# Mixture-of-experts layer: experts ranked by token count on the chip and run in 13 units instead of 16 fixed pairs

## The chip, the cores and the metric

The kernel runs on one core of a Trainium2 chip. The metric is the device time of one execution in microseconds (us); of a set of runs the median counts. The core has TensorE (matrix products; PE in the rows, with PEld for its weight loads), VectorE (DVE), ScalarE (ACT), GpSimd (POOL) and SyncE (SP, which here issues the large loads), and 16 DMA engines that carry all transfers.

## What is computed

One inference step of a two-layer network (`DEPTH = 2`) on 128 context tokens and 128 latent tokens. Each layer has a block of three token mixers, and then a mixture of 32 experts in which each of the 256 tokens goes to its 4 best experts. Only the second part is touched. All values are float32.

```python
D_MODEL, N_EXPERTS, TOP_K, D_EXPERT = 1024, 32, 4, 512

def _moe(h, p):
    t = h.reshape(b * n, d)
    logits = t @ p['router_w'] + p['router_b']
    top_v, top_i = lax.top_k(logits, TOP_K)
    w_top = jax.nn.softmax(top_v, axis=-1)
    combine = einsum('tk,tke->te', w_top, one_hot(top_i, N_EXPERTS))
    def expert(acc, e):
        w1, b1, w2, b2, ce = e
        gu = t @ w1 + b1                       # (1024 x 1024)
        gate = minimum(gu[:, :D_EXPERT], 7.0)
        up = clip(gu[:, D_EXPERT:], -7.0, 7.0)
        act = (up + 1.0) * (gate * sigmoid(1.702 * gate))
        return acc + ce[:, None] * (act @ w2 + b2), None   # w2: 512 x 1024
```

An expert's weights are 4 MB of w1 and 2 MB of w2. Every expert gets tokens, so all 32 are loaded in each layer.

## The kernel before

After the mixers, TensorE computes the router's logits; VectorE takes each token's four best experts, and from running counts the position of each token within each expert. Experts are worked through in **pairs**. A pair has 128 slots, 64 for each expert: a 0/1 matrix `S_s` (tokens by slots, made by `tokens_onehot`) gathers the tokens of both by matrix products (`gather`), and `SC_s` (from `combine_onehot`) scatters the weighted results back onto all tokens.

On TensorE one pair is, in `pair(q)`: products with the first half of w1 (L811, `part` 0, which counts up `g1_mm[0]`), with the second half (`part` 1, `g1_mm[1]`), the gather of the next pair (L770), four transposes of the activations (L819), the products with w2 (L837, `g2_mm`), the scatter (L845) and the next pair's biases (L778). The two experts of a pair lie in two column halves of the array: a weight tile is 128 rows by 64 slots, the expert's weights stream past it 512 columns at a time, and the halves of the two experts work at the same time.

An expert with more than 64 tokens gets further slots in an **extra** pair. VectorE finds these during pair 0 (L1542 to L1588: tables of 16 extras by 32 experts, in rows of 512 elements), and raises `routed`. The extra pairs run after the first three pairs, and the 13 fixed ones follow; the number of pairs is thus 16 and the extra ones, and all engines but SP run them in one hardware loop from pair 1 (TensorE from pair 2).

Weights come in **parts** of 2 MB: two of w1 and one of w2 for each expert, each of them one DMA issued by SP in program order. The buffers are the six slots of `ring`, which the mixers' weights use too: slots 0 and 1 for the first half of w1, 2 and 3 for the second, 4 and 5 for w2. SP waits on `g1_mm[0]`, `g1_mm[1]` or `g2_mm` before it issues the load into a slot that TensorE has finished with (`load_part`, L405). Two further buffers, `more`, hold the first halves of w1 of pair 1 once per layer. Eight parts are so loaded before pair 0 starts. At the end of a layer SP loads the next layer's first weights into the six slots as they come free.

Of the kernel before, what the change touches and what calls it, by code (L numbers as in the profile page):

```python
# [27 lines left out]
G = 2  # L28
# [13 lines left out]
FIRST = 3  # L42
# [17 lines left out]
C_PIDX, C_KK, C_EIDX, C_EPS, C_FOLD = 704, 705, 721, 753, 754  # L60
NC = 786
# [23 lines left out]
def merge_slot(kind, b, ch):  # L85

    return {"gate": S_WM[b][ch // 4], "proj": S_WO[b], "out": S_OUT + ch // 4}[kind]

# [6 lines left out]
def build(nc, x_in, cond_in, consts, vecs, rows, ada_w, w_in, w_q_b, w_kv_b, lru_gate_w, w_o_mla, w_o_lru,  # L95
# [3 lines left out]
    with ctx:  # L99
# [41 lines left out]
        eidi = sb("eidi", [P, MAX_EXTRA], I32)  # L141
        ps = ctx.enter_context(nc.psum_tensor("ps", [P, 8, 512], F32))

        def at(off, *dims):
# [8 lines left out]
            if len(dims) == 4:  # L153
# [61 lines left out]
        xtra = at(T0 + 436, N_EXP)  # L215
        tend = at(T0 + 468, N_EXP)
        tbeg = at(T0 + 500, N_EXP)
        npf = at(T0 + 532, 2)
        cmp8 = at(T0 + 534, 8)
        psub = at(T0 + 542, MAX_EXTRA)  # L220
        NTAB = N_EXP + MAX_EXTRA + 2
        pmT = at(T0 + 558, G, NTAB)
        cwT = at(T0 + 658, G, NTAB)
        eidf = at(T0 + 758, NTAB)
        ctT = at(T0 + 808, NT)
        lpart = ctT
        K0 = T0 + 1064
        sel, tmpx, tmpy = (at(K0 + 512 * i, MAX_EXTRA, N_EXP) for i in range(3))
        assert K0 + 3 * 512 <= 19776

# [34 lines left out]
                             "ct_mm", "ct_evac", "routed"))  # L265
        disp, xt_a, xt_v = (sem(n) for n in ("disp_rdy", "xt_evac_a", "xt_evac_v"))
# [101 lines left out]
        with nc.Fori(0, L) as l:  # L368
            with nc.Block() as block:

                @block.sync
                def _(sp_):
# [35 lines left out]
                    def pair(experts, waits, order=range(RING)):  # L408

                        srcs = [expert_parts(e) for e in experts]  # L410
                        for j in order:
                            s, v = waits[j]
                            sp_.wait_ge(s, v)
                            load_part(j, srcs[j % 2][j // 2])

                    def freed(pairs_before):

                        return [(g1_mm[0], pairs_before)] * 2 + [(g1_mm[1], pairs_before)] * 2 + \
                            [(g2_mm, pairs_before * 2)] * 2
# [5 lines left out]
                    free = [consumed(pos) for pos in last_pos]  # L425
                    pair((0, 1), free, order[:3])
                    sp_.wait_ge(pv_mm, 12)
                    sp_.wait_ge(out_done, 16 * 5)
                    load_part(1, expert_parts(3)[0], more[1], more_arr[1])
                    pair((0, 1), free, order[3:])  # L430
                    sp_.wait_ge(f_mm, len(MERGE))
                    sp_.wait_ge(f_dv, 32)
                    load_part(0, expert_parts(2)[0], more[0], more_arr[0])
# [4 lines left out]
                    sp_.wait_ge(routed, 1)  # L438
                    n_extra = sp_.value_load(meta[0:1, 0:1], min_val=0, max_val=MAX_EXTRA // 2)
                    with sp_.If(n_extra > 0):  # L440
                        with sp_.Fori(0, n_extra) as q:
                            e = [sp_.value_load(eidi[0:1, bass.ds(q * 2 + i, 1)], min_val=0, max_val=N_EXP - 1)
                                 for i in range(2)]
                            two = sp_.value_load(both[0:1, bass.ds(q, 1)], min_val=0, max_val=1)
                            with sp_.If(two > 0):
                                pair(e, freed(q + FIRST))
                            with sp_.Else():

                                srcs = expert_parts(e[0])
                                for j, (s, v) in enumerate(freed(q + FIRST)):  # L450
                                    sp_.wait_ge(s, v)
                                    if j % 2 == 0:
                                        load_part(j, srcs[j // 2])
                                    else:
                                        sp_.sem_inc(arr[j], 16)
# [1254 lines left out]
```

## Time and profile before

| | us |
|---|---|
| median of 3 runs | 1813.56 (1812.35 to 1814.66) |
| the profiled execution, own time | 1813.54 |
| its span in the trace | 1811.9 |
| TensorE busy | 1737.7 (96% of the span) |
| VectorE busy, ScalarE busy | 606.1, 275.9 |
| experts of layer 0, first product to last bias | 386.85 to 912.86 |
| experts of layer 1 | 1280.81 to 1804.98 |

The profile is of one execution. Times in the rows count from the span's start; the own time is 1.6 us longer than the span. Matrix products on TensorE are pipelined, so a row of the timeline that holds many of them is read by its start and by the start of the next row. In a row of products `128*64` is the weight tile, `128x512` the output. A product in float32 appears as two instructions.

### The profile page before, as it was taken

To read this page: it belongs to the slowest core of one execution; us is meant where nothing else is said; L and a number is where in the kernel's file an instruction comes from. 1 tells how busy PE (TensorE), PEld (TensorE's weight loads), DVE (VectorE), ACT (ScalarE), POOL (GpSimd) and SP (SyncE) were. 2 spreads that over 40 slices of the span, in tenths; PEclk is the share of its full clock that TensorE was granted. 3 is DMA by queue.
4 is the path that set the end of the run, shared out by engine and by line. 5 is a ranking of instruction groups with operands and counts; after the bars stand their busy time and mean duration, and the time that the engine had idled before them with its cause. 6 is when DMAs were issued, how large, how long until landed. Compare 5 with 4: busy or idle time off the path is not lost. (4 is left out here: it accounts for less than half of the span.)

```text
span 1811.9 us, 22234 instructions
## 1 busy us (share of the span) xinstructions
PE 1737.7 (96%) x8560; PEld 1002.6 (55%) x8560; DVE 606.1 (33%) x1733; ACT 275.9 (15%) x611; POOL 3.8 (0%) x6
## 2 busy tenths in 40 slices
PE   3999999989999999999979999999899999999998
PEld 1756787844444444444438468877544444444444
DVE  1368235261222222121233863443512121212122
ACT  2133222020000000000030422212100000000001
POOL 0000000000000000000000000000000000000000
PEclk9999999989999999999989999999999999999999
DMA  9754633956699999999976455368566999999994
GB/s 324 276 182 151 239 141 108 362 206 255 243 421 412 417 414 416 417 413 418 405 261 225 145 179 202 140 211 352 201 269 272 417 414 419 411 420 408 421 411 175
DMA packets 100557, 551.52 MB, mean 304 GB/s; under 512 B 12753, under 2 KB 15569, under 8 KB 75025
## 3 DMA queue, kind: packets, MB, share of 16 engines
q1 hardware_dynamic: 91376, 546.20, 75.8%
q10 hardware_dynamic: 9120, 4.53, 1.0%
q8 instruction: 36, 0.59, 0.1%
q14 instruction: 25, 0.20, 0.0%
HBM read 548.31 MB, written 2.40 MB: 304 GB/s over the span
## 5 line engine op out<-in xcount | busy, mean ns | idle before, releaser
L811 PE MATMUL ps<-ring,arena 128*64 128x512 f32 x2112 | 460.6, 594 | 0.0
L811 PEld LDWEIGHTS ps<-ring,arena 128*64 128x64 f32 x2112 | 148.7, 137 | 307.6 <-issue 306.1
L837 PE MATMUL ps<-ring,arena 128*64 128x512 f32 x1088 | 241.0, 595 | 0.0
L622 PE MATMUL ps<-hT,ring 128*128 128x256 f32 x768 | 171.4, 379 | 0.0
L770 PEld LDWEIGHTS ps<-arena 128*128 128x128 f32 x1152 | 139.1, 198 | 36.2 <-issue 26.0
L1518 DVE TENSOR_SCALAR arena<-cst,arena 128x64 f32<-128x64 f32 x136 | 33.4, 310 | 373.0 <-PE ps L811 372.9
L770 PE MATMUL ps<-arena 128*128 128x128 f32 x1152 | 148.5, 284 | 8.2 <-DVE arena L1508 8.2
L622 PEld LDWEIGHTS ps<-hT,ring 128*128 128x128 f32 x768 | 144.1, 190 | 19.4 <-issue 1.0
L837 PEld LDWEIGHTS ps<-ring,arena 128*64 128x64 f32 x1088 | 75.0, 137 | 141.7 <-issue 141.7
L622 PE MATMUL ps<-arena,ring 128*128 128x256 f32 x640 | 144.6, 380 | 2.9 <-ACT arena L1020 1.6
L1082 ACT ACTIVATE arena<-arena 128x512 f32<-128x512 f32 x34 | 21.4, 630 | 753.4 <-DVE arena L1596 753.4
L622 PEld LDWEIGHTS ps<-arena,ring 128*128 128x128 f32 x640 | 118.8, 190 | 19.0 <-issue 2.7
L845 PE MATMUL ps<-arena 128*128 128x256 f32 x544 | 126.5, 386 | 0.0
L583 PE MATMUL ps<-ring,hT 128*128 128x512 f32 (+1 forms) x320 | 121.4, 540 | 1.9 <-DVE hT L1182 1.9
L845 PEld LDWEIGHTS ps<-arena 128*128 128x128 f32 x544 | 100.5, 190 | 39.9 <-issue 27.6
L1608 DVE COPY arena<-ps 128x512 f32<-128x512 f32 x34 | 23.5, 692 | 222.8 <-PE ps L837 222.8
L583 PEld LDWEIGHTS ps<-ring,hT 128*128 128x128 f32 x320 | 58.0, 192 | 63.8 <-issue 62.5
L1596 DVE TENSOR_SCALAR arena<-ps 128x512 f32<-128x512 f32 x34 | 23.5, 691 | 149.4 <-PE ps L811 149.4
L492 PE MATMUL ps<-arena,cst 128*128 128x256 f32 x64 | 20.2, 485 | 38.9 <-PEq L334 28.3
L589 PE MATMUL ps<-hT,ring 128*128 128x256 f32 x256 | 55.6, 379 | 0.0
L589 PEld LDWEIGHTS ps<-hT,ring 128*128 128x128 f32 x256 | 48.5, 190 | 6.5
L999 ACT ACTIVATE arena<-ps,bmh 128x256 f32<-128x256 f32 x48 | 22.8, 475 | 142.4 <-PE ps L622 137.2
(266 smaller groups left out, 1317.3 us busy)
## 6 DMA issues: line engine op xcount, KB each, us to landing
ring<-exp_w_dram SPq DMA_DIRECT2D x194, 2048.0 KB, 10.9
ring<-ada_w_dram SPq DMA_DIRECT2D x24, 2048.0 KB, 8.6
ring<-w_in_dram SPq DMA_DIRECT2D x12, 2048.0 KB, 10.1
ring<-w_merge_dram SPq DMA_DIRECT2D x12, 2048.0 KB, 9.0
ring<-w_out_dram SPq DMA_DIRECT2D x4, 2048.0 KB, 10.9
arena<-exp_w_dram SPq DMA_DIRECT2D x4, 2048.0 KB, 20.0
ring<-w_o_lru_dram SPq DMA_DIRECT2D x2, 2048.0 KB, 7.7
ring<-w_o_mla_dram SPq DMA_DIRECT2D x2, 2048.0 KB, 19.3
```

The source lines that it names most:

```text
L583: last = mm(ps[:, bank, 0:w], hT[:, k, half * P:(half + 1) * P], slot[:, k, :], start=k == 0, stop=k == KC - 1)
L589: last = mm(ps[:, bank, c * NT:(c + 1) * NT], slot[:, k, ch * P:(ch + 1) * P], hT[:, k, :], start=k == 0, stop=k == KC - 1)
L622: last = mm(out, slot[:, k, cols], src[:, k, :], start=k == 0, stop=k == nk - 1)
L770: last = mm(ps[:, 2 + k // 4, (k % 4) * P:(k % 4 + 1) * P], X2[:, g, k * P:(k + 1) * P], S_s[:, g, :], start=g == 0, stop=g == 1)
L811: last = mm(ps[c, h, :], xTg[:, 4 * part + k, c], w[i][:, k, h * 512:(h + 1) * 512], start=False, stop=True, skip_group_check=True)
L837: last = mm(ps[c, 2 + h, :], actT[:, f, c], w[i][:, f, h * 512:(h + 1) * 512], start=f == 0, stop=f == 3)
L845: last = mm(ps[:, 4 + k // 2, (k % 2) * NT:(k % 2 + 1) * NT], O_s[:, k * P:(k + 1) * P], SCT[:, :], start=first and k % 2 == 0, stop=True, ...
L999: A(tg[:, ch, :], merge_ps(f), ACT.Tanh, bias=bmh[:, 8 * b + ch:8 * b + ch + 1], scale=0.5).then_inc(f_ac, 1)
L1082: A(sig_s, gate_s, ACT.Sigmoid, scale=ALPHA).then_inc(sig_a, 1)
L1518: V.tensor_scalar(SC_s[:, g, SLOTS * i:SLOTS * (i + 1)], cst[:, C_IOTA:C_IOTA + SLOTS], pmT[:, g, bass.ds(t + i, 1)], cwT[:, g, bass.ds(t ...
L1596: V.tensor_scalar(gate_s, ps[:, 0, :], LIMIT, None, ALU.min).then_inc(gate_v, 1)
L1608: V.tensor_copy(O_s[:, 512:1024], ps[:, 3, :]).then_inc(o_v, 1)
```

## The change

- The experts are taken by rank. Experts 0 to 3 keep fixed places, so that work can start before the ranks are known; the other 28 are ordered by token count, the fullest first (`ranks`, on VectorE, with `cnt` scaled and the expert's number as tie-breaker).
- `UNITS` lists 13 units: nine pairs of 64 slots each, one unit of 96 and 32 slots (the fullest ranked expert and the last one), and three units of four experts with 32 slots each. A unit still has 128 slots. Units 0 to 11 are written out one after another on every engine; unit 12 and the extras run in the hardware loop. Extras come last, after unit 12.
- In units with 32 or 96 slots the array is split into four column groups of 32 (`tiles`); the group of an expert streams that expert's weights. With 96 slots three groups stream the same weights.
- The ring has eight buffers (six slots and `more`); part n goes into buffer n mod 8, and SP waits for the use of part n - 8. From unit 2 on SP reads the expert's number from `eidi` into a register before the unit's loads, after `routed`. In unit 12 and the extras the parts use slots 2 and 3, 4 and 5, 0 and 1.
- The tables of positions and weights by rank are no longer built on VectorE in 512-element rows but by small matrix products with a selection matrix `selT`: `table_parts` stands between the two halves of w1 of unit 0, `tables` behind the second. The transposition of the combine weights (L786 before) is in `table_parts`, so the biases of unit 0 follow the gather directly. TensorE waits for `routed` before the scatter of unit 0.
- `tokens_onehot` and `combine_onehot` take one operation each for all equal-sized experts of a unit; `combine_onehot` multiplies `S_s` by the weights.

```diff
+UNITS = (pair_at(0), pair_at(2), ((4, 96), (31, 32)), pair_at(5), pair_at(7), quad_at(19), pair_at(9), pair_at(11),
+         quad_at(23), pair_at(13), pair_at(15), quad_at(27), pair_at(17))
+NU = len(UNITS)
+CAPACITY = [w for _, w in sorted(e for unit in UNITS for e in unit)]
+LOOPED = NU - 1
+PARTS = [(u, kind, i) for u, unit in enumerate(UNITS[:LOOPED]) for kind in range(3) for i in range(len(unit))]
+BUFS = RING + 2
+LOOP_SLOTS = ((2, 3), (4, 5), (0, 1))
...
+                    def part_freed(n):
+                        u, kind, _ = PARTS[n]
+                        sp_.wait_ge(*((g1_mm[0], u + 1), (g1_mm[1], u + 1), (g2_mm, 2 * u + 2))[kind])
+                    def load_static(n, e):
+                        b = n % BUFS
+                        if n >= BUFS:
+                            part_freed(n - BUFS)
+                        src = part_source(PARTS[n][1], e)
+                        if b < RING:
+                            load_part(b, src)
+                        else:
+                            load_part(b, src, more[b - RING], more_arr[b - RING])
...
-                    pair((4, 5), freed(1), (0, 1))
-                    pair((2, 3), freed(1), range(2, RING))
-                    pair((4, 5), freed(2), range(2, RING))
+                    sorted_from = part_number(2, 0, 0)
+                    for n in range(BUFS, sorted_from):
+                        load_static(n, fixed_expert(n))
                     sp_.wait_ge(routed, 1)
+                    for u in range(2, LOOPED):
+                        ids = [sp_.value_load(eidi[0:1, t:t + 1], min_val=0, max_val=N_EXP - 1) for t, _ in UNITS[u]]
+                        for kind in range(3):
+                            for i, e in enumerate(ids):
+                                load_static(part_number(u, kind, i), e)
...
+                    def tiles(u):
+                        widths = [w for _, w in UNITS[u]]
+                        if widths == [SLOTS, SLOTS]:
+                            return [(i, slice(SLOTS * i, SLOTS * (i + 1))) for i in range(2)]
+                        owner = [i for i, w in enumerate(widths) for _ in range(w // 32)]
+                        return [(i, slice(32 * n, 32 * n + 32)) for n, i in enumerate(owner)]
...
+                    for u in range(LOOPED):
+                        experts = tiles(u)
+                        w1_products(u, 0, experts, part_weights(u, 0))
+                        if u == 0:
+                            table_parts()
+                        w1_products(u, 1, experts, part_weights(u, 1))
+                        if u == 0:
+                            tables()
+                        pe.wait_ge(disp, u + 2)
+                        gather(range(6))
+                        act_transposes(u)
+                        w2_products(u, experts, part_weights(u, 2))
+                        if u == 0:
+                            pe.wait_ge(routed, 1)
+                        scatter(u, first=u == 0)
+                        biases()
```

The order of instructions shows three places. On TensorE, first the start of unit 0 in each layer. Before: the gather of pair 0, the transposition of the combine weights (L786), the biases, all 32 products with w1, the next gather.

```order
L770 MATMUL ps<-arena 128x128 x16
L786 MATMUL ps<-cst,arena 32x128 x2
L778 MATMUL ps<-arena 128x512 x2
L811 MATMUL ps<-ring,arena 64x512 x32
L770 MATMUL ps<-arena 128x128 x12
```

After, down to the gather of unit 1 (L827 is the gather, L835 the biases, L849 the products with w1, L917 to L926 `table_parts`, L934 to L941 `tables`):

```order
L835 MATMUL ps<-arena 128x512 x2
L849 MATMUL ps<-ring,arena 64x512 x16
L917 MATMUL ps<-cst,arena 32x128 x2
L919 MATMUL ps<-cst,arena 32x128 x2
L925 MATMUL ps<-arena,cst 32x1 x2
L926 MATMUL ps<-arena,cst 128x1
L849 MATMUL ps<-ring,arena 64x512 x16
L934 MATMUL ps<-arena 128x50
L936 MATMUL ps<-arena,cst 128x16
L934 MATMUL ps<-arena 128x50
L936 MATMUL ps<-arena,cst 128x16
L939 MATMUL ps<-arena 128x50 x2
```

Two products have left the place ahead of the biases, and fourteen small ones (with L941 behind the last row) stand within and behind the products with w1. Second, on TensorE, a whole pair before (pair 1), in the same names:

```order
L811 MATMUL ps<-arena 64x512 x16
L811 MATMUL ps<-ring,arena 64x512 x16
L770 MATMUL ps<-arena 128x128 x12
L819 MATMUL ps<-cst,arena 128x128 x4
L770 MATMUL ps<-arena 128x128 x4
L824 MATMUL ps<-cst,arena 128x128 x2
L837 MATMUL ps<-ring,arena 64x512 x16
L845 MATMUL ps<-arena 128x256 x8
L778 MATMUL ps<-arena 128x512 x2
```

After, unit 2, the first with column groups of 32:

```order
L849 MATMUL ps<-ring,arena 32x512 x32
L849 MATMUL ps<-arena 32x512 x32
L827 MATMUL ps<-arena 128x128 x12
L858 MATMUL ps<-cst,arena 128x128 x4
L827 MATMUL ps<-arena 128x128 x4
L863 MATMUL ps<-cst,arena 128x128 x2
L873 MATMUL ps<-ring,arena 32x512 x32
L885 MATMUL ps<-arena 128x256 x8
L835 MATMUL ps<-arena 128x512 x2
```

Only the counts of L849 and L873 double, with half the columns each; a unit of four experts has the same rows. Third, on SP, the loads around the wait for `routed`. Before, these are the last parts of pairs 1 and 2:

```order
L405 ISA [waits w1_mm1]
L405 DMA ring<-exp_w1_dram 128x4096
L405 ISA [waits w2_mm]
L405 DMA ring<-exp_w2_dram 128x4096
L405 ISA [waits w2_mm]
L405 DMA ring<-exp_w2_dram 128x4096
L439 TENSOR_LOAD meta [waits routed]
L439 ISA x2
```

After, the last part of unit 1 and the first three of unit 2:

```order
L432 ISA [waits w1_mm1]
L432 DMA ring<-exp_w2_dram 128x4096
L481 TENSOR_LOAD eidi [waits routed]
L481 ISA x2
L481 TENSOR_LOAD eidi
L481 ISA x2
L432 ISA [waits w2_mm]
L432 DMA ring<-exp_w1_dram 128x4096
L432 ISA [waits w2_mm]
L432 DMA ring<-exp_w1_dram 128x4096
L432 ISA [waits w1_mm0]
L432 DMA arena<-exp_w1_dram 128x4096
```

The wait for `routed` has moved ahead of the loads of unit 2, register loads stand ahead of each unit's parts, and a part waits for whichever stage used its buffer last (here w1 parts wait for `w2_mm`).

## Rows read from the trace of the kernel before

**Rows 1.** Page, part 1: span; part 5: one group that runs once a pair.

```profile
span 1811.9 us, 22234 instructions
...
L1608 DVE COPY arena<-ps 128x512 f32<-128x512 f32 x34 | 23.5, 692 | 222.8 <-PE ps L837 222.8
```

**Rows 2.** Timeline of TensorE, one pair (start, duration, line, shape, count).

```profile
579.33 13.95 PE L811 MATMUL ps<-ring,arena 128*64 128x512 f32 x64
593.21 2.94 PE L770 MATMUL ps<-arena 128*128 128x128 f32 x24
...
597.91 7.09 PE L837 MATMUL ps<-ring,arena 128*64 128x512 f32 x32
604.93 3.72 PE L845 MATMUL ps<-arena 128*128 128x256 f32 x16
...
609.64 13.96 PE L811 MATMUL ps<-ring,arena 128*64 128x512 f32 x64
```

**Rows 3.** Waits of SP's queue: total us, times, longest.

```profile
SPq L405 <- PE ps L811: 564.7, 62, 30.8
```

**Rows 4.** Loads at L405: issue times, and times from issue to landing.

```profile
L405 SPq DMA_DIRECT2D ring<-exp_w_dram x2: 333/333/333, 605.2 to 605.7; - x2
...
DMA to landing us min/median/max: 8.7/10.9/13.1
...
L405 SPq DMA_DIRECT2D ring<-exp_w_dram x2: 333/333/333, 617.0 to 617.6; - x2
...
DMA to landing us min/median/max: 7.6/9.8/11.9
```

**Rows 5.** Stretches: length, busy times, granted clock, DMA share, GB/s (last three columns).

```profile
823.10:853.40 30.30, 30.30 (x156) 14.35 (x154) 6.69 (x17) 2.21 (x4) 0.00 (x0) 1.00 1.00 415
...
505.00:520.00 15.00, 15.00 (x74) 7.58 (x75) 2.19 (x4) 0.98 (x2) 0.00 (x0) 1.00 1.01 434
0.00:20.00 20.00, 0.00 (x0) 0.00 (x0) 0.61 (x3) 3.30 (x3) 0.20 (x4) 1.00 0.94 328
```

**Rows 6.** Page, part 6: issues of expert weights, KB each, us to landing.

```profile
ring<-exp_w_dram SPq DMA_DIRECT2D x194, 2048.0 KB, 10.9
...
arena<-exp_w_dram SPq DMA_DIRECT2D x4, 2048.0 KB, 20.0
```

**Rows 7.** Timeline of TensorE: the modulation products of layer 1, in four column groups.

```profile
929.67 7.08 PE L501 MATMUL ps<-ring,cT 128*32 128x512 f32 x64
```

**Rows 8.** Timeline of TensorE, pair 0 and the start of pair 1, layer 0.

```profile
384.62 0.62 PE L786 MATMUL ps<-cst,arena 128*32 128x128 f32 x4
385.79 1.13 PE L778 MATMUL ps<-arena 32*128 32x512 f32 x4 [0.55 <-ACT arena L1071]
386.85 13.95 PE L811 MATMUL ps<-ring,arena 128*64 128x512 f32 x64
403.27 4.45 PE L770 MATMUL ps<-arena 128*128 128x128 f32 x24 [2.46 <-DVE arena L1508]
...
420.87 4.44 PE L858 MATMUL ps<-arena 32*128 32x256 f32 x16
425.23 9.60 PE L811 MATMUL ps<-arena 128*64 128x512 f32 x32
```

**Rows 9.** Stretches in pairs 0 and 1 of layer 0; columns as in rows 5.

```profile
400.00:405.00 5.00, 2.54 (x12) 1.74 (x9) 4.16 (x16) 0.63 (x1) 0.00 (x0) 0.80 1.00 429
...
425.00:430.00 5.00, 5.00 (x13) 1.48 (x14) 0.00 (x0) 0.00 (x0) 0.00 (x0) 0.50 0.64 272
```

**Rows 10.** Timeline of VectorE, first operation behind a register load.

```profile
400.77 0.18 DVE L1586 COPY arena<-cst 128x26 f32 x1 [1.07 <-issue]
```

**Rows 11.** Timeline of TensorE: last biases of layer 0, first and last rows of layer 1's experts.

```profile
911.73 1.13 PE L778 MATMUL ps<-arena 32*128 32x512 f32 x4
...
1280.81 13.95 PE L811 MATMUL ps<-ring,arena 128*64 128x512 f32 x64
...
1803.85 1.13 PE L778 MATMUL ps<-arena 32*128 32x512 f32 x4
```

More of the change, by code:

```diff
@@ L406, in load_part, with part_source @@
                             arr[slot] if signal is None else signal, 16)
[L408 to L419, printed above, removed]
+                    def part_source(kind, e):
+                        return expert_parts(e)[kind]
@@ new lines, in w1_products @@
+                    def w1_products(q, part, experts, weights):
+                        for k in range(4):
+                            for h in range(2):
+                                for i, c in experts:
+                                    last = mm(ps[c, h, :], xTg[:, 4 * part + k, c],
+                                              weights[i][:, k, h * 512:(h + 1) * 512], start=False,
+                                              stop=True, skip_group_check=True)
+                        last.then_inc(g1_mm[part], 1)
@@ L863, in _ @@
-                    with pe.Fori(2, pairs) as q:
-                        pair(q)
+                    for u in range(LOOPED):
[14 more added lines that the diff above has]
+                        biases()
+                        if u == 0:
+                            pe.wait_ge(ld_b2, 16)
+                            for k in range(KC):
+                                mm(ps[:, 4 + k // 2, (k % 2) * NT:(k % 2 + 1) * NT], b2[0:N_EXP, k * P:(k + 1) * P],
+                                   ctT[0:N_EXP, :], start=False, stop=True, skip_group_check=True)
@@ new lines, in _ @@
+                    with pe.Fori(LOOPED, pairs) as q:
+                        experts = tiles(LOOPED)
+                        w1_products(q, 0, experts, loop_weights(q, 0))
+                        w1_products(q, 1, experts, loop_weights(q, 1))
+                        pe.wait_ge(disp, q + 2)
+                        gather(range(6))
+                        act_transposes(q)
+                        w2_products(q, experts, loop_weights(q, 2))
+                        scatter(q)
+                        biases()
@@ L1087, in pair @@
                         A(O_s[:, 0:512], ps[:, 2, :], ACT.Copy).then_inc(o_a, 1)
[L1089 removed]
+                    for u in range(LOOPED):
+                        pair(u)
                     act.wait_ge(routed, 1)
[L1091 to L1092 removed]
+                    pairs = act.value_load(meta[0:1, 1:2], min_val=NU, max_val=NU + MAX_EXTRA // 2)
+                    with act.Fori(LOOPED, pairs) as q:
                         pair(q)
```

379 lines of the change are left out of this document (217 added, 162 removed).

## The prediction

> **What bounds the kernel now.** I read the page first, for how often the expert work runs: the copy at L1608 stands once in a pair, and it ran 34 times [rows 1], so each layer has 17 pairs, 16 fixed and one extra. Then the timeline of one pair [rows 2]: the rows on TensorE join without a gap, 13.95 us for w1, then 4.7 us to the start of w2 (w1 ends at 593.2, w2 starts at 597.9), 7.0 for w2, 4.7 for scatter and biases (604.9 to 609.6). From start to start it is 30.31 us. TensorE never waits there for a load; SP waits for TensorE, 564.7 us in all for w1 products [rows 3]. So TensorE sets the pace. The loads, though, are close behind. Each expert part of 2 MB is 2.097 million bytes; two parts issued at 605.2 and 605.7 landed 8.7 and 13.1 us later, at 613.9 and 618.8, and the next two, issued at 617.0 and 617.6, at 624.6 and 629.5 [rows 4]. With a queue, landings are 4.9 us apart (428 GB/s); the part issued at 617.0 found the queue nearly done and began 2.7 us after its issue (624.6 - 4.9 = 619.7), which leaves a hole of 0.9 us. Six parts thus take 29.4 us of a pair's 30.3. The whole pair shows 415 GB/s at a DMA share of 1.00 [rows 5], because TensorE asks for no more. Taking work off TensorE is worth little more than 3% of a pair before the loads take over; taking loads away is worth more.
>
> **What is loaded and run.** 194 + 4 parts were issued [rows 6]: 66 experts, 33 per layer, so each extra pair holds one expert. The router of the reference, worked out for the reference's own inputs, agrees: in layer 0 only expert 1 (76 tokens) exceeds 64, in layer 1 only expert 29 (80). By rank, expert 29 gets the unit with 96 slots and needs no extra. Expert 1 is one of the four with a fixed place, and keeps its extra. No expert in a 32-slot place has more than 27 tokens, none in a 64-slot place more than 60 apart from expert 1. So layer 0 goes from 17 units to 14, layer 1 from 17 to 13, and the loads from 66 experts to 65.
>
> **A unit of four experts on TensorE.** It has twice the weight tiles of a pair, with half the columns. The nearest row is the modulation, the same shape with four different weight streams: 64 products in 7.08 us [rows 7], 110 ns each, against 13.95/64 = 218 ns for two streams [rows 2]. So 128 products take 14.1 us as a pair's 64 take 13.95, and I give all units 30.31 us, 13 x 30.31 = 394 us for a layer. Their loads do not shrink: 12 parts x 4.9 = 58.8 us for four experts. **The bound changes from TensorE to the loads.** What the three large units save on TensorE becomes waiting there, and the pairs between let the loads run ahead by what eight buffers hold.
>
> **The head of unit 0.** L786 and its wait leave the place before the biases: these start when L786 did, 384.62 instead of 385.79 [rows 8], 1.2 us earlier in each layer. In pair 0 the gather waited 2.46 us for VectorE's tables and then took 4.45 us instead of 2.94 at a granted clock of 0.80 [rows 8, 9]; that goes. In its place stand 14 small products. L786's four instructions are two such, 0.62 us, so 14 x 0.31 = 4.3 us; the bounds are 0 (beside VectorE's activation chain) and 8.6 (the same at half clock). VectorE's rank chain, some 15 operations of about 0.2 us, lies under the first half of w1. The b2 products (4.4 us) and the slow 9.60 us behind them, at a clock of 0.50, remain [rows 8, 9]. The register loads on SP, about 1.07 us each [rows 10], lie in its waits; four before a large unit are 4.3 us while several parts are queued, so I charge nothing. If that cover is gone, they become the rival below. The one-hots fall from ten operations to three a unit on VectorE, which is off the path: no gain.
>
> **The sum for one layer.** I walk through the parts: a part begins when the one before it has landed, or 3.0 us after the use of its buffer ends (0.3 to the issue, 2.7 to the start), whichever is later. Eight parts lie ready. Counted from the first w1 product of unit 0:
> - Part 14 needs the buffer of part 6, which unit 1's first half of w1 uses: 30.3 (unit 0) + 4.3 (small products) + 4.4 (b2) + 2.6 (slow clock, 9.60 less 7.0) + 7.0 + 3.0 = 51.6. The parts 8 to 13 have landed before.
> - From there to part 89, the last of unit 11, are 76 parts x 4.9 = 372.4 us, with four holes of 0.9 while units 1 to 4 are still paced by TensorE as now: 427.6.
> - Then the tail: 0.1 to the wake-up, 7.0 for w2, 1.5 for the low clock after the wait (the 4.45 less 2.94 above), 4.7 for scatter and biases, and unit 12, whose parts have landed meanwhile, 30.3: **471.3 us**.
>
> Layer 0 adds its extra behind that, 30.3, loaded under unit 12: 501.6. Before, layer 0 took 386.85 to 911.73 + 1.13, which is 526.0; layer 1 1280.81 to 1803.85 + 1.13, 524.2 [rows 8, 11]. The gain is 24.4 + 52.9, and 2 x 1.2 at the heads: 79.7 us. What lies around (the update of x, the next layer's first loads) stays. The profiled execution's own time is 1813.54, 1.6 us over its span and equal to the median of 1813.56. **Forecast: 1734 us.**
>
> Ends of the terms: at 434 GB/s, as 15 us of rows 5 show, a part takes 4.83 us, -7 us in all after the longer holes; at the pair's 415 it takes 5.05, +16. I take 4.9, the spacing of landings itself. The small products move it by -9 to +9. Quad stages longer by a quarter, from starting after each wait at a low clock as in rows 9, cost +17. Together about 1718 to 1760.
>
> **A rule against this.** Expert loads moved at 434 GB/s for 15 us on end [rows 5]. The Trainium skill (DMA: Bandwidth & Descriptors, "Where 436 GB/s comes from") says that transfers from HBM to SBUF are bound at about 358 GB/s per core. By it, an estimate, a part takes 5.86 us, a layer some 74 us more, and the change ends near 1880, slower than before. The trace already runs above that figure, so the measurement decides; a rate that falls in longer stretches stays as a rival.
>
> **The rivals.**
> - *The large units take longer on TensorE.* If four column groups run only two abreast (218 ns as in rows 2), or every stage behind a wait stays at half clock, w1 and w2 take 21 us more in each of the four units with groups of 32. The same walk then gives 34 us more per layer: 1802. Against it speaks the 110 ns of rows 7; for it, that TensorE now waits some 20 us in a large unit. Half that effect gives 1769. The Trainium skill (TensorE: Matmul & The Clock Gate, "HAM oscillation — how this bites in real kernels") describes groups of products that each start cold after a wait for a DMA; rows 9 show one such case, and the sum has it once, at the end. 10%, most of it at the half effect.
> - *Not four groups side by side at all: slower.* Then a 32-column product costs 2 x 218 = 436 ns, and w1 and w2 of such a unit 63 us more. TensorE alone needs 13 x 30.31 + 4 x 63 + 11.3 = 657 us in a layer: 1734 + 2 x 186 = 2106. It turns slower once a unit takes 57 us, which is 248 ns a product. Rows 7 are against it. 1%.
> - *The loads do not hold 4.9 us without a pause: slower.* The opening 20 us moved only 328 GB/s at a share of 0.94 [rows 5], though in smaller pieces; that is 6.39 us a part. Per layer 76 x 1.49 - 3.6 + 8 (unit 12 waits too) = 118: 1969. The point is 5.47 us a part (383 GB/s), where 2 x (76 x 0.57 - 3.6) eats the 79.7. Expert parts stand at 415 to 434. 3% beyond the point, 2% between 5.1 and it (1755 to 1810).
> - *The ranking doesn't remove layer 1's extra*, by a wrong place or capacity: one unit of 30.3 us back, 1764. The counts say no. 4%.
> - *Register loads come into the open* on SP: 28 in a layer x 1.07 = 30 us, 1794 if nothing covers them. SP sits waiting most of a pair today. 2%.
>
> **How the numbers follow.** The forecast with its terms' bounds, 1718 to 1760, has 78%. The range needs 80% and takes in the half effect of the first rival and the extra: 1718 to 1769. A measurement of this kernel can tell 0.2% from no change, 3.6 us. All cases end faster but the two slower ones (4%); nearly none falls within 0.2% (1%). Faster 95%.
>
> **What would show it.** Right: 27 executions of the pair's copy instead of 34 (14 + 13) and 195 expert parts; four-group products at about 110 ns; from unit 5 on waits of TensorE for loads, some 20 us in a large unit and none in unit 12, and DMA at about 428 GB/s without a hole; layers of about 502 and 471 us. Wrong: a mean near 218 ns; TensorE without waits in the large units; holes between parts behind register loads; a rate under 400 GB/s while parts are queued.

## The result, and the profile after

The changed kernel takes 1729.94 us (median of four runs, 1728.60 to 1733.86) against 1813.01 for the kernel before in the same comparison: a ratio of 0.9544, with a 95% interval of 0.9527 to 0.9561. It is 83.1 us faster. The forecast was 1734.0, a gain of 79.7. The profiled execution took 1728.60 us, with a span of 1726.9.

The page of the changed kernel, parts 1, 2, 5 and 6, to be held against [rows 1, 6]:

```profile
span 1726.9 us, 20608 instructions
PE 1556.0 (90%) x8298; PEld 905.1 (52%) x8298; DVE 514.6 (30%) x1415; ACT 260.9 (15%) x585; POOL 3.8 (0%) x6
...
GB/s 336 294 159 144 295 69 130 355 187 321 419 419 412 428 426 428 427 427 427 317 261 313 150 152 269 70 156 324 218 298 412 420 412 427 428 427 428 428 427 200
...
L1763 DVE COPY arena<-ps 128x512 f32<-128x512 f32 x27 | 18.7, 692 | 228.2 <-PE ps L873 228.2
...
ring<-exp_w_dram SPq DMA_DIRECT2D x151, 2048.0 KB, 20.6
...
arena<-exp_w_dram SPq DMA_DIRECT2D x44, 2048.0 KB, 15.6
```

The copy at L1763 stands once in a unit and ran 27 times, 14 + 13, in place of 34 [rows 1]. 151 + 44 = 195 expert parts were issued in place of 198 [rows 6], and the usual time from issue to landing has grown from 10.9 to 20.6 us: a longer queue of loads now stands before the DMA engines. The GB/s row shows it: in each layer's expert work (slices 11 to 19 and 31 to 39) it climbs from 412–420 to 426–428 and stays there.

The waits, TensorE's and those of SP's queue (total us, times, longest), beside [rows 3]:

```profile
PE ps L849 <- DMA ring<-exp_w_dram: 66.2, 10, 11.3
PE ps L873 <- DMA ring<-exp_w_dram: 37.6, 6, 7.5
...
SPq L432 <- PE ps L849: 523.6, 50, 29.1
...
SPq L481 <- DVE eidi L1737: 4.4, 2, 2.2
```

Before, TensorE did not wait for an expert load at all. Now it waits 66.2 + 37.6 = 103.8 us for w1 parts (L849) and w2 parts (L873). SP's wait for the ranked ids (L481) comes once in a layer and is short.

The timeline of TensorE in layer 0 (start, duration, line, operation, shape, count, and in brackets the idle time before it and what ended it): unit 2, the first with four column groups, which finds its weights ready; unit 8, the second large unit behind the first pairs; the end of unit 11 and the start of unit 12:

```profile
450.10 7.07 PE L849 MATMUL ps<-ring,arena 128*32 128x512 f32 x64
456.99 7.05 PE L849 MATMUL ps<-arena 128*32 128x512 f32 x64
...
650.56 1.07 PE L849 MATMUL ps<-arena 128*32 128x512 f32 x2 [2.92 <-DMA ring<-exp_w_dram]
...
670.14 8.76 PE L849 MATMUL ps<-ring,arena 128*32 128x512 f32 x64 [9.57 <-DMA ring<-exp_w_dram]
...
689.94 1.06 PE L873 MATMUL ps<-arena 128*32 128x512 f32 x2 [6.32 <-DMA ring<-exp_w_dram]
...
703.67 13.95 PE L849 MATMUL ps<-ring,arena 128*64 128x512 f32 x64
...
808.94 1.07 PE L873 MATMUL ps<-arena 128*32 128x512 f32 x2 [6.08 <-DMA ring<-exp_w_dram]
...
818.20 3.72 PE L885 MATMUL ps<-arena 128*128 128x256 f32 x16
...
822.91 13.95 PE L849 MATMUL ps<-ring,arena 128*64 128x512 f32 x64
```

Unit 2: 128 instructions with 32 columns take 14.1 us, 110 ns each, just as a pair's 64 take 13.95. (The prediction counts instructions as products; a product in float32 is two of them.) Unit 2 holds two experts, of 96 and 32 slots, and so two weight streams. Four streams stand first in unit 5; its first half of w1, which finds its weights ready, in the line view (count, ns min/median/max, first and last start):

```profile
L849 PE MATMUL ps<-arena x32: 592/592/617, 541.0 to 547.5; 128*32 128x512 f32 x32
...
L849 PE MATMUL ps<-ring,arena x32: 592/592/617, 541.0 to 547.5; 128*32 128x512 f32 x32
```

These 64 instructions take 7.1 us, again 110 ns each. Unit 8 waits three times, 2.92 + 9.57 + 6.32 = 18.8 us; unit 11 waits 22.2 in the same way. The pair behind each runs without a wait, unit 12 too. That is the pattern of the forecast, but for unit 5, which waits only 10.1 us.

The loads, first as stretches (columns as in [rows 5]; the last three are granted clock, DMA share, GB/s), then as issues at L432 with their times to landing, which answer to [rows 4]:

```profile
590.00:700.00 110.00, 91.19 (x531) 40.50 (x528) 17.18 (x30) 6.63 (x12) 0.00 (x0) 0.89 1.01 427
700.00:800.00 100.00, 83.90 (x470) 37.84 (x469) 14.20 (x26) 5.04 (x9) 0.00 (x0) 0.93 1.01 428
```

```profile
L432 SPq DMA_DIRECT2D ring<-exp_w_dram x2: 332/332/333, 717.8 to 718.3; - x2
...
DMA to landing us min/median/max: 26.9/29.1/31.3
...
L432 SPq DMA_DIRECT2D arena<-exp_w_dram x2: 332/332/333, 729.5 to 730.1; - x2
...
DMA to landing us min/median/max: 24.9/27.1/29.3
```

These four parts land at 744.7, 749.6, 754.4 and 759.4: 4.9 us apart, without the hole of 0.9 that the prediction read from [rows 4]. TensorE is busy 91 of 110 us, the DMA engines all the time. The bound has passed from TensorE to the loads.

The ends of the layers on the same timeline, answering to [rows 8, 11]:

```profile
383.01 7.09 PE L849 MATMUL ps<-ring,arena 128*64 128x512 f32 x32
...
882.48 1.13 PE L835 MATMUL ps<-arena 32*128 32x512 f32 x4
...
1249.54 7.09 PE L849 MATMUL ps<-ring,arena 128*64 128x512 f32 x32
...
1718.80 1.13 PE L835 MATMUL ps<-arena 32*128 32x512 f32 x4
```

From the first w1 product to the end of the last bias, layer 0 takes 883.61 - 383.01 = 500.6 us and layer 1 takes 1719.93 - 1249.54 = 470.4. The forecasts were 501.6 and 471.3, the times before 526.0 and 524.2.

### The profile page after: what moved, and what is told of

It reads as the page before. It is cut to its first block and busy times, and to the rows that moved or that the text cites. A ratio compares the mean times of both kernels' runs of the same rounds, so it can differ in the third digit from the quotient of the medians.

```text
span 1726.9 us, 20608 instructions
## 1 busy us (share of the span) xinstructions
PE 1556.0 (90%) x8298; PEld 905.1 (52%) x8298; DVE 514.6 (30%) x1415; ACT 260.9 (15%) x585; POOL 3.8 (0%) x6
## 5 line engine op out<-in xcount | busy, mean ns | idle before, releaser
L849 PE MATMUL ps<-ring,arena 128*64 128x512 f32 (+1 forms) x1856 | 371.2, 632 | 50.4 <-DMA ring<-exp_w_dram 50.4
L849 PEld LDWEIGHTS ps<-ring,arena 128*64 128x64 f32 (+1 forms) x1856 | 111.9, 132 | 266.2 <-issue 266.2
L679 PE MATMUL ps<-hT,ring 128*128 128x256 f32 x768 | 171.4, 379 | 0.0
L873 PE MATMUL ps<-ring,arena 128*64 128x512 f32 (+1 forms) x736 | 161.9, 634 | 0.0
L679 PEld LDWEIGHTS ps<-hT,ring 128*128 128x128 f32 x768 | 144.1, 190 | 19.4 <-issue 1.0
L873 PE MATMUL ps<-arena 128*32 128x512 f32 (+1 forms) x384 | 98.2, 670 | 37.6 <-DMA ring<-exp_w_dram 37.6
L827 PEld LDWEIGHTS ps<-arena 128*128 128x128 f32 x928 | 111.5, 197 | 23.5 <-issue 20.5
L827 PE MATMUL ps<-arena 128*128 128x128 f32 x928 | 119.0, 283 | 2.6 <-DVE arena L1650 2.6
L1657 DVE TENSOR_TENSOR arena<-arena 128x256 f32<-128x256 f32 (+2 forms) x29 | 11.6, 407 | 318.1 <-PE ps L849 318.1
L885 PE MATMUL ps<-arena 128*128 128x256 f32 x432 | 100.5, 386 | 0.0
L885 PEld LDWEIGHTS ps<-arena 128*128 128x128 f32 x432 | 79.8, 190 | 31.9 <-issue 22.1
L849 PE MATMUL ps<-arena 128*32 128x512 f32 (+1 forms) x384 | 79.1, 642 | 15.8 <-DMA ring<-exp_w_dram 15.8
L1763 DVE COPY arena<-ps 128x512 f32<-128x512 f32 x27 | 18.7, 692 | 228.2 <-PE ps L873 228.2
L873 PEld LDWEIGHTS ps<-arena 128*32 128x32 f32 (+1 forms) x384 | 27.7, 135 | 99.0 <-issue 99.0
L873 PEld LDWEIGHTS ps<-ring,arena 128*64 128x64 f32 (+1 forms) x736 | 45.7, 131 | 62.5 <-issue 62.5
L849 PEld LDWEIGHTS ps<-arena 128*32 128x32 f32 (+1 forms) x384 | 21.5, 122 | 70.5 <-issue 70.5
## 6 DMA issues: line engine op xcount, KB each, us to landing
ring<-exp_w_dram SPq DMA_DIRECT2D x151, 2048.0 KB, 20.6
```

The source lines that it names most:

```text
L679: last = mm(out, slot[:, k, cols], src[:, k, :], start=k == 0, stop=k == nk - 1)
L827: last = mm(ps[:, 2 + k // 4, (k % 4) * P:(k % 4 + 1) * P], X2[:, g, k * P:(k + 1) * P], S_s[:, g, :], start=g == 0, stop=g == 1)
L849: last = mm(ps[c, h, :], xTg[:, 4 * part + k, c], weights[i][:, k, h * 512:(h + 1) * 512], start=False, stop=True, skip_group_check=True)
L873: last = mm(ps[c, 2 + h, :], actT[:, f, c], weights[i][:, f, h * 512:(h + 1) * 512], start=f == 0, stop=f == 3)
L885: last = mm(ps[:, 4 + k // 2, (k % 2) * NT:(k % 2 + 1) * NT], O_s[:, k * P:(k + 1) * P], SCT[:, :], start=first and k % 2 == 0, stop=True, ...
L1763: V.tensor_copy(O_s[:, 512:1024], ps[:, 3, :]).then_inc(o_v, 1)
```

## The experiments

The theory: from about unit 5 on the loads set the pace; a part costs 4.9 us; what the large units save on TensorE comes back as waits, as far as the ring's look-ahead doesn't carry the savings over to the next pairs. The rivals that the trace alone does not exclude: the ranking does all of it and the large units nothing; the gain hangs on something else, register loads or clock; the waits are a thing of the places that the large units stand in. All ratios are against the kernel before. Layer times are read as above, from each kernel's profiled execution; waits are TensorE's for expert loads, both layers together. x_halfw2 and x_noreg do not compute the reference's output.

| kernel | median us | ratio (95%) | layer 0 | layer 1 | waits |
|---|---|---|---|---|---|
| before | 1813.01 | 1 | 526.0 | 524.2 | none |
| after | 1729.94 | 0.9544 (0.9527–0.9561) | 500.6 | 470.4 | 103.8 |
| x_pairs | 1771.45 | 0.9770 (0.9754–0.9786) | 521.9 | 491.6 | none |
| x_six | 1797.23 | 0.9906 (0.9889–0.9923) | 533.8 | 504.1 | 167.8 |
| x_halfw2 | 1646.57 | 0.9083 (0.9057–0.9108) | 458.7 | 428.4 | 41.2 |
| x_noreg | 1729.39 | 0.9535 (0.9520–0.9551) | 500.6 | 470.9 | 106.1 |
| x_b2late | 1723.66 | 0.9498 (0.9485–0.9511) | 497.3 | 467.5 | 101.0 |
| x_order | 1723.09 | 0.9495 (0.9482–0.9508) | 501.2 | 467.4 | 100.5 |
| x_warm | 1727.52 | 0.9521 (0.9508–0.9534) | 498.9 | 469.4 | 93.8 |
| x_all | 1715.16 | 0.9447 (0.9434–0.9460) | 492.9 | 462.5 | 82.5 |
| a_again (after once more) | 1730.84 | 0.9542 (0.9529–0.9555) | 500.6 | 470.8 | 105.6 |
| b_again (before once more, one execution) | 1812.86 | – | 524.4 | 525.9 | none |

**Ranking without large units.** The table of units holds pairs only, 16 in a layer; slots, ranking and ring stay.

```diff
-UNITS = (pair_at(0), pair_at(2), ((4, 96), (31, 32)), pair_at(5), pair_at(7), quad_at(19), pair_at(9), pair_at(11),
-         quad_at(23), pair_at(13), pair_at(15), quad_at(27), pair_at(17))
+UNITS = (pair_at(0), pair_at(2), ((4, 96), (31, 32))) + tuple(pair_at(t) for t in range(5, 31, 2))
```

> The changed kernel with a different table of units: ranks, ring of eight and everything else kept, but 16 units (two fixed pairs, the one of 96 and 32 slots, thirteen pairs) and no unit of four experts. Theory of the prediction (units of four shift the bound from TensorE to the loads): TensorE sets the pace again at 30.31 us a unit, 17 units in layer 0 and 16 in layer 1, no waits for loads; about 24 us more per layer than the changed kernel, 1777 us. Rival (the gain came from the ranks' missing extra, the head of unit 0 and the larger ring, and the units of four only trade work for waits): within 8 us of the changed kernel, 1722 to 1738.

It took 1771.45, and both layers are 21 us longer than after, where 24 was expected. The GB/s row of this kernel's page:

```profile
GB/s 333 283 182 144 260 120 98 394 166 358 417 412 421 411 419 412 420 408 348 259 260 302 156 144 286 94 100 392 163 358 420 409 422 409 420 412 419 413 373 119
```

The rate in the expert work is that of a pair before [rows 5], 408 to 422 GB/s, and no wait for a load stands in the list of TensorE's waits: TensorE sets the pace again. Its layer 1 can be added up from pieces: 16 units of 30.31 [rows 2], 3.1 for the small products and 3.5 for b2 (both as measured after, see below) are 491.6, the time measured. So the change's 83 us are two halves: 41.6 us from ranking and what comes with it (32.6 us of that in layer 1, whose extra unit is gone; 4.1 in layer 0, where only pair 0's wait with its slow gather and the slow clock behind b2 could go; the rest lies ahead of the layers and between them), and 41.5 us from the large units. The eight buffers were not taken out of this kernel by themselves; but TensorE waited for no load with six before, so pairs alone leave them little to give. The rival that the ranking does it all falls.

**Six buffers in place of eight.** The ring keeps its six places; the two further buffers and the two parts loaded ahead into them go.

```diff
-BUFS = RING + 2
-LOOP_SLOTS = ((2, 3), (4, 5), (0, 1))
+BUFS = RING
+LOOP_SLOTS = ((0, 1), (2, 3), (4, 5))
...
-                    load_static(RING + 1, fixed_expert(RING + 1))
...
-                    load_static(RING, fixed_expert(RING))
```

> The changed kernel with the ring cut from eight buffers to the six slots (the two further buffers unused, eight parts ready at the start become six). Theory (loads bound the units of four, and the ring decides how far they run ahead): while four parts of a unit of four are in use only two buffers can fill, holes appear between the loads; the same walk through the parts gives 29 us more per layer, about 1788 us. Rival (the ring only matters for the start; six slots were enough before): about 10 us more per layer at most, 1730 to 1750.

It took 1797.23: both layers are 33 us longer than after, where 29 was expected. TensorE's waits, and one stretch in layer 0 (columns as above):

```profile
PE ps L847 <- DMA ring<-exp_w_dram: 113.9, 19, 13.8
PE ps L871 <- DMA ring<-exp_w_dram: 53.9, 6, 9.8
```

```profile
700.00:760.00 60.00, 49.88 (x298) 25.28 (x292) 10.47 (x17) 4.42 (x8) 0.00 (x0) 0.94 0.94 388
```

The waits grow by 64 us, and in the stretch the rate falls to 388 GB/s at a DMA share of 0.94: the loads pause. Work and units are the same, so 67 of the 83 us are lost without the longer look-ahead. Six buffers with large units are slower even than eight with pairs alone (1797 against 1771); six with pairs alone were not run. Why the loss was 33 and not 29 a layer wasn't followed further.

**Half of each w2 part not loaded.** In units 2 to 11 only the first half of the w2 matrix is loaded (the products run unchanged on what lies in the buffer), so the loads shrink and TensorE's work does not.

```diff
+                        if PARTS[n][1] == 2 and PARTS[n][0] >= 2:
+                            half = src.rearrange("o (p k) n -> p (o k) n", p=P)[:, 0:2, :]
+                            dst = ring[:, b, 0:2048] if b < RING else more[b - RING][:, 0:2048]
+                            sp_.dma_start(dst.rearrange("p (k n) -> p k n", k=2), half).then_inc(
+                                arr[b] if b < RING else more_arr[b - RING], 16)
+                            return
```

> The changed kernel with only the first half of each w2 part loaded in units 2 to 11 (the output is then not the reference's). Theory (loads are the bound from unit 5 on): waits of TensorE for loads nearly vanish, 43 us less per layer, about 1644 us; TensorE's own work, 13 x 30.3 us and the head of unit 0, is the floor near 1630. Rival (units of four are long on TensorE itself, or the clock after waits holds it back): within 10 us of the changed kernel.

It took 1646.57; the layers fall by 41.9 and 42.0 us, against an expected 43. TensorE's waits for loads, in this kernel:

```profile
PE ps L855 <- DMA ring<-exp_w_dram: 41.2, 11, 8.3
```

The waits fall from 103.8 to 41.2 and the time by 83.4 us with not one product less: the waits of TensorE are the loads', and bytes are what sets the end. The other 21 us is TensorE's busy time in the layers, which falls from 867.2 to 845.8 for the same instructions, because fewer stages run at the lower clock (mean granted clock 0.97 and 0.98 in place of 0.94). That the waits nearly vanish was a miss: 41.2 us are left.

**No register loads.** In units 2 to 11 the ids of the experts come from the table of places in place of a load from SBUF into SP's registers (so the routed units load experts by place and not by rank, as many bytes).

```diff
-                        ids = [sp_.value_load(eidi[0:1, t:t + 1], min_val=0, max_val=N_EXP - 1) for t, _ in UNITS[u]]
+                        ids = [t for t, _ in UNITS[u]]
```

> The changed kernel with the register loads of the experts' numbers in units 2 to 11 left out on SP: the loads take experts by their place in the table instead of by rank (the output is then not the reference's). Theory of the prediction (register loads lie in SP's waits and cost nothing): within 3 us of the changed kernel. Rival (they delay the issue of loads): 26 fewer per layer at about 1 us each, up to 50 us less, 1680 us.

It took 1729.39 against 1729.94, layers of 500.6 and 470.9. The register loads cost nothing that can be measured; SP has time for them behind the queued parts, as it sits 523.6 us in its waits for w1 products.

**The b2 products later.** The 16 small products that add b2 move from unit 0, where TensorE sets the pace, to unit 5.

```diff
-                        if u == 0:
+                        if u == 5:
```

> The changed kernel with the 16 products with b2 moved from behind unit 0 to behind unit 5, the first unit of four. Theory (units 0 to 4 are paced by TensorE and hold the buffers, from unit 5 on the loads set the pace, so TensorE's work costs its full time before unit 5 and nothing after): 3.5 us less per layer, about 7 us less in all, 1723 us. Rival (the loads set the pace from the start of the experts, or TensorE does throughout): no difference, within 2 us.

It took 1723.66, 3.3 and 2.9 us less per layer than after where 3.5 was expected. On the timeline of this kernel the products have their old length at the new place:

```profile
582.22 3.61 PE L965 MATMUL ps<-arena 32*128 32x256 f32 x16
```

There they don't make the layer longer: TensorE's waits are 2.8 us less and its busy time 3.4 us less, both layers together. In unit 0 they delayed the release of the buffers, and with it every part behind: part 14 lands 48.2 us after the first w1 product in layer 0, in place of 51.8 after.

**The large units earlier.** The units of four stand at places 2, 5 and 11 in place of 5, 8 and 11, so that the loads set the pace from the third unit on.

```diff
-UNITS = (pair_at(0), pair_at(2), ((4, 96), (31, 32)), pair_at(5), pair_at(7), quad_at(19), pair_at(9), pair_at(11),
-         quad_at(23), pair_at(13), pair_at(15), quad_at(27), pair_at(17))
+UNITS = (pair_at(0), pair_at(2), quad_at(19), ((4, 96), (31, 32)), pair_at(5), quad_at(23), pair_at(7), pair_at(9),
+         pair_at(11), pair_at(13), pair_at(15), quad_at(27), pair_at(17))
```

> The changed kernel with the units in another order: units of four experts at places 2, 5 and 11 instead of 5, 8 and 11. Theory (total loads decide, the order only sets how many holes the loads have while TensorE paces them): 2 to 3 us less per layer, about 1725 us. Rival (the spacing of units of four is what lets the loads run ahead; two of them close together wait in full): about 10 us more per layer, 1750 us.

It took 1723.09, where 1725 was expected. Fewer holes are in the loads: added up from the landings of parts 15 to 89, the pauses beyond 4.89 us a part are 3.8 and 4.3 us in the two layers, against 7.0 and 6.7 after. In the profiled execution, its slowest at 1727.13, layer 1 is 3.0 us shorter than after and layer 0 is 0.6 longer. The timeline and a stretch of layer 0 of this execution account for that:

```profile
417.00 4.95 PE L965 MATMUL ps<-arena 32*128 32x256 f32 x16
421.88 9.09 PE L849 MATMUL ps<-arena 128*64 128x512 f32 x32
```

```profile
420.00:425.00 5.00, 5.00 (x13) 1.99 (x13) 0.00 (x0) 0.00 (x0) 0.00 (x0) 0.50 0.87 374
```

The clock fell to half (0.50, the level of 1.2 GHz) during and behind the b2 products, which made these two rows 4.95 and 9.09 us long in place of 3.61 and 7.09: 3.3 us. That is the slow clock of [rows 8, 9], which the execution of after did not have; without it, an estimate, the layer would be 2.7 shorter than after.

**Work in the last wait.** Before the w2 products of unit 11, whose wait for loads is the last in the trace after, TensorE multiplies data that nobody reads.

```diff
+                        if u == LOOPED - 1:
+                            pe.wait_ge(sct_ev, u + 1)
+                            for _ in range(6):
+                                mm(ps[:, 1, :], ident, X2[:, 0, 0:512], start=True, stop=True, skip_group_check=True)
```

> The changed kernel with six products whose result nobody uses (128 columns of weights, 512 columns of data, 5 us in all) in front of the w2 products of unit 11, where TensorE waits some 6 us for a load. Theory (behind that wait w2 runs at the low clock and takes 9.2 us instead of 7.0, and this is the last wait, so it counts): w2 there 7.0 us, 2 us less per layer, 1726 us. Rival (the time is decided by the loads up to the end, so the clock costs nothing): no difference, within 1.5 us.

It took 1727.52. First the line view of the w2 products of unit 11 after (count, ns min/median/max, first and last start) and a stretch in it; then the same of this kernel, with the filling products above:

```profile
L873 PE MATMUL ps<-ring,arena x32: 592/592/1062, 809.0 to 817.7; 128*32 128x512 f32 x32
...
810.00:815.00 5.00, 5.00 (x35) 1.31 (x28) 0.00 (x0) 0.10 (x1) 0.00 (x0) 0.65 1.00 419
```

```profile
804.84 5.42 PE L960 MATMUL ps<-arena,cst 128*128 128x512 f32 x12 [0.47 <-ACT arena L1213]
...
L873 PE MATMUL ps<-ring,arena x32: 592/592/617, 810.2 to 816.7; 128*32 128x512 f32 x32
...
810.00:815.00 5.00, 5.00 (x49) 1.56 (x52) 0.00 (x0) 0.60 (x1) 0.00 (x0) 1.00 1.00 423
```

The stage takes 7.0 us in place of 9.3, and the granted clock in it is 1.00 in place of 0.65: an engine that has worked until the load lands starts at full clock. The stage's gain is plain, 2.3 us in layer 0 and 2.6 in layer 1. The layers, though, are only 1.7 and 1.0 us shorter than after. Part of the gain comes back in unit 12, which has a wait that after did not have:

```profile
829.62 7.09 PE L849 MATMUL ps<-ring,arena 128*64 128x512 f32 x32 [0.62 <-DMA ring<-exp_w_dram]
```

After, the second of the two parts that this half needs landed at 828.2 and TensorE came to it at 829.9, so there were 1.7 us to gain before the loads bind again. In the whole kernel the gain is at the edge of what can be told: 0.9521 (to 0.9534) against 0.9542 (from 0.9529) for after in its second comparison.

**All three edits** (b2 late, large units early, work in the last wait).

> The three edits before this one together: b2 behind unit 5, units of four at places 2, 5 and 11, six unused products before w2 of unit 11. If they add: 7 + 5 + 4 us less than the changed kernel, about 1714 us. Rival (the first two fill the same holes in the loads): about 1720 us.

It took 1715.16 us, a ratio of 0.9447 (0.9434 to 0.9460) against the kernel before and 0.9% under the changed kernel; layers of 492.9 and 462.5. The three gains, each against after in ratio times 1813 (8.0, 8.5 and 3.8 us), add up to 20; together they give 17. It is the fastest version of this study that loads every weight; the GB/s row of its page:

```profile
GB/s 334 302 151 154 261 67 171 305 241 311 418 428 428 428 428 427 427 427 427 333 261 314 159 154 245 67 186 287 259 295 408 427 427 428 428 427 428 427 427 219
```

The rate is at 427–428 from the twelfth slice on, two slices earlier than after.

**Both kernels once more.** In the first traces the router of layer 0 ended 3 us earlier after than before, ahead of anything that the change touches; this asks whether that belongs to the change.

> The kernel before, unchanged, profiled once more: does its first product with w1 in layer 0 always start at 386.9 us? In the changed kernel it started 3.8 us earlier, of which the shorter way from the router explains 0.8. If the other 3 us are only the run (the clock and the first loads at the start), this trace starts anywhere between 383.5 and 387. Rival (the change moved something ahead of the router): 386.5 to 387.2 again.

> The changed kernel, unchanged, timed in five rounds as a base for the last four runs: 1730 us, with layers of about 500.6 and 470.4 us again; first product with w1 between 381.5 and 384.6 us, as the runs of its relatives showed.

The router's product in the timelines of before and of after, then of before once more and of after once more:

```profile
369.90 4.86 PE L737 MATMUL ps<-hT,rw 128*32 128x256 f32 x16 [3.56 <-DVE hT L1182]
```

```profile
366.84 4.42 PE L794 MATMUL ps<-hT,rw 128*32 128x256 f32 x16 [3.56 <-DVE hT L1307]
```

```profile
366.90 4.42 PE L737 MATMUL ps<-hT,rw 128*32 128x256 f32 x16 [3.56 <-DVE hT L1182]
...
377.13 6.79 PE L770 MATMUL ps<-arena 128*128 128x128 f32 x32 [1.78 <-DVE arena L1508]
```

```profile
369.42 4.86 PE L794 MATMUL ps<-hT,rw 128*32 128x256 f32 x16 [3.56 <-DVE hT L1307]
```

Before comes early this time, and after comes late: the 3 us differ from run to run of either kernel, and are no part of the change. The first w1 product of before starts at 386.08, inside the theory's stretch and under the rival's; that of after at 384.66, at the upper end of what was expected. The times, 1812.86 and 1730.84, and layer 1 after (470.8) repeat.

## Why the prediction was right, and where its terms were off

**The bound and the walk through the parts held.** The prediction said that loads would take over, that a part costs 4.9 us, that TensorE waits from unit 5 on, some 20 us in a large unit, and not in unit 12. The trace after has 10.1 us in unit 5, half of what was said, 18.8 in unit 8, 22.2 in unit 11 and none in unit 12. Half w2 parts (x_halfw2) confirm the cause, six buffers (x_six) the part that the look-ahead has, and x_pairs the size of what is left without large units.

**The terms of a layer,** forecast and trace of layer 0. The opening is set together from its rows, in the timeline of unit 0:

```profile
390.03 0.62 PE L917 MATMUL ps<-cst,arena 128*32 128x128 f32 x4
...
391.48 7.09 PE L849 MATMUL ps<-ring,arena 128*64 128x512 f32 x32
398.50 0.42 PE L934 MATMUL ps<-arena 32*128 32x50 f32 x2
...
400.14 2.94 PE L827 MATMUL ps<-arena 128*128 128x128 f32 x24
...
416.25 3.61 PE L965 MATMUL ps<-arena 32*128 32x256 f32 x16
419.79 7.09 PE L849 MATMUL ps<-arena 128*64 128x512 f32 x32
```

- Small products: 391.48 - 390.03 and 400.14 - 398.50, 3.1 us together; forecast 4.3. The gather behind them takes 2.94 without a wait, as forecast; the 2.46 + 1.5 us of pair 0 [rows 8] are gone.
- b2: 419.79 - 416.25, 3.5 us; forecast 4.4, the length that it had in the trace before [rows 8].
- Slow clock behind b2: none, 7.09 and not 9.60; forecast 2.6. This is the term that was mis-sized most. Both layers of before and of b_again have it (8.37 to 9.81 us); of the sixteen layers of the changed kernel and its relatives with b2 behind unit 0, only layer 0 of x_order does. The prediction took away pair 0's wait for VectorE but kept this slow clock, which stood some 20 us behind that wait; whether the two belong together was not tested.
- So part 14 was issued at 427.1 and landed 7.7 us later (the rows below); it began some 4.9 before that, at about 429.9, which is 46.9 us after the first w1 product; forecast 51.6.

```profile
L432 SPq DMA_DIRECT2D arena<-exp_w_dram x2: 333/333/333, 427.1 to 427.6; - x2
...
DMA to landing us min/median/max: 7.7/9.9/12.1
```

- From there to the start of unit 11's w2 at 808.94 are 379.1 us for 76 parts; forecast 376.1 (372.4, four holes of 0.9 and the 0.1 to the wake-up). Where the rate is highest a part is at 4.9 as said; the loss is in the holes, 7.0 us in place of 3.6. Of these, 5.0 lie at or ahead of part 33, the last of unit 5's first half and so in the stretch that TensorE still paces, and 2.0 behind it; in layer 1 it is 3.3 of 6.7.
- The last w2 behind its wait: 818.20 - 808.94, 9.3 us; forecast 7.0 + 1.5 = 8.5.

The opening was 4.7 us too dear, the walk 3.0 and the last stage 0.8 too cheap, which leaves about -1: the layers came out 0.9 to 1.0 us under the forecast. That they hit so closely is thus in part luck, for the terms' errors cancel. Of the 3.4 us by which the gain exceeds its forecast, the two layers make 1.9; the rest is less than the runs of one kernel differ by (1728.60 to 1733.86).

**The heads.** L786's way out of the path was put at 1.2 us in each layer. From the router to the first w1 product layer 0 gains 0.8 (16.95 us before, 16.17 after) and layer 1 gains 1.7 (17.85, 16.17), 2.5 us in all against 2.4. This too is luck in part. In layer 1 the gather between them takes 5.47 us in both kernels, and the 1.7 is L786's 1.2 and 0.5 from a shorter wait of the gather (1.78 us before, 1.28 after), which the prediction did not have. In layer 0 the gather takes 5.47 us after and 3.84 before, which costs 1.6 us of the same gain; the products around the router give 0.7 back.

**The rule against the change.** Over 210 us on end (590 to 800) the expert loads moved at 427 and 428 GB/s. The Trainium skill (DMA: Bandwidth & Descriptors, "Where 436 GB/s comes from") would have bound them at about 358 GB/s; the trace disagrees, and the measurement decides. The prediction's estimate by that figure, a time near 1880, did not come either.

**The rivals.** *Large units twice as long on TensorE*: no for the four groups, 110 ns each in unit 5. But the half of this rival that came from the clock did happen in part: w1 stages behind a wait take 8.7 to 10.0 us, as at 670.14, in place of 7.05, and w2 of unit 11 takes 9.3. The prediction had the loss once in its sum and came out right with that: the walk needs no such loss in the other stages, so a stage that runs 2 us longer while the loads set the pace only shortens the next wait. x_warm shows 1.7 and 1.0 us a layer for the last one. The Trainium skill (TensorE: Matmul & The Clock Gate, "HAM oscillation — how this bites in real kernels") describes groups of products that start cold after each wait for a DMA; the rows here agree, but by the walk only the last one's cost reaches the end. (The case that the prediction names from [rows 9] came after a wait for VectorE, not for a DMA.) *Loads that don't hold their pace*: 427–428. *Ranking that fails*: 27 executions of the copy. *Register loads*: nothing, by x_noreg.

**What the prediction did not see** is that its opening terms could be had back. It priced unit 0's small work on the path that sets the end, which was right, and x_b2late and x_order show that about 3 us a layer each go away when the work or the large units change place.

## What to carry to other kernels

Where units paced by TensorE and units paced by loads stand in one chain, price the whole stretch by bytes over the sustained rate, and see whether the buffers carry the loads over the TensorE-paced units: here two more buffers were worth 67 us of the large units' kernel, and with six it was slower than pairs with eight (six with pairs was not run). In a chain paced by loads, what counts here was the work ahead of the first load-paced part, the holes between the loads, and the work behind the last wait; move small work out of the first and the last into the waits. A stage that starts cold behind a wait costs time only where no further wait absorbs it, and making it faster gains no more than the slack of the loads behind it (1.7 us here).

## What the runs showed of the hardware

- One core kept 427–428 GB/s from HBM for 210 us, with parts of 2 MB landing 4.9 us apart and several queued.
- Four column groups of 32 with four different weight streams in fp32 run side by side: 110 ns an instruction (unit 5) against 218 with two groups of 64.
- TensorE's granted clock in the short products around the router and b2 differs from run to run of the same kernel: the first gather of layer 0 took 5.47 us in after and 3.84 in a_again, 3.84 in before and 6.79 in b_again. The w1 half behind b2 took 7.09 us at a clock of 1.00, or 9.09 (x_order) and 9.60 (before) with the clock at 0.50 in it. Why one run has it and another has not stays open.
